# RWKV key norms summed token-major and turned back, in the input projection of a hybrid encoder layer

## The reference

```python
prev = jnp.pad(ub, ((0, 0), (1, 0), (0, 0)))[:, :-1]
ub = ub + (prev - ub) * mu                       # token shift
r, k, v, w_low, a_low, g_low = _split(ub, B_COLS)
...
a = jax.nn.sigmoid(a0 + a_low @ a_up)
...
kk = _l2norm(_heads(k * k_k, RWKV_HEADS))        # u * rsqrt(sum(u * u) + 1e-6) over the 64 columns of a head
k = k * (1.0 + (a - 1.0) * k_a)
...
bonus = jnp.sum(r_h * k_h * r_k, -1, keepdims=True) * v_h
```

## Time and profile before

| | |
|---|---|
| median of 3 runs | 2105.22 us (2103.75 to 2105.71) |
| time of the profiled execution | 2102.6 us |
| its span, first to last instruction | 2100.8 us |
| mean granted TensorE clock | 0.974 |
| TensorE busy | 1967.7 us, 94% |
| VectorE busy | 1078.3 us, 51% |
| ScalarE, GpSimd busy | 567.8 us, 558.6 us |

### The profile page before, as it was taken

How to read it: one execution, slowest core, us unless ns; L and a number is a source line. 1 busy time by engine, 2 the same in 40 slices (tenths; PEclk the granted TensorE clock), 3 DMA queues, 4 the chain that set the end, 5 groups by cost and what they waited for, 6 DMA issues and landing times. The chain is left out here.

```text
span 2100.8 us, 29168 instructions
## 1 busy us (share of the span) xinstructions
PE 1967.7 (94%) x11664; PEld 1575.3 (75%) x11664; DVE 1078.3 (51%) x1354; ACT 567.8 (27%) x884; POOL 558.6 (27%) x353
## 2 busy tenths in 40 slices
PE   5998979999999999899888999999999999999994
PEld 4876758767788887777767777888888888888883
DVE  3665764468429900566657644724334243443437
ACT  2443332334421121333331121321121211212112
POOL 3111112121122322433314473422121221212113
PEclk9999989999999999899999999999999999999997
DMA  5243566135563393566464461211121211211002
GB/s 144 53 70 89 130 151 164 51 76 140 148 173 100 97 218 107 147 189 197 119 215 131 134 207 51 61 61 50 41 60 30 60 32 58 60 30 60 30 20 80
DMA packets 328054, 211.84 MB, mean 101 GB/s; under 512 B 154349, under 2 KB 298349, under 8 KB 325905
## 3 DMA queue, kind: packets, MB, share of 16 engines
q1 hardware_dynamic: 251760, 156.33, 27.3%
q10 hardware_dynamic: 75568, 54.04, 9.0%
q0 software_dynamic: 624, 0.05, 0.2%
HBM read 151.27 MB, written 59.06 MB: 100 GB/s over the span
## 5 line engine op out<-in xcount | busy, mean ns | idle before, releaser
L154 PE MATMUL bank<-xhi,w_hi 128*128 128x512 f32 x976 | 396.3, 406 | 2.9 <-DVE xlo L920 2.9
L155 PE MATMUL bank<-xlo,w_hi 128*128 128x512 f32 x976 | 387.6, 397 | 0.0
L156 PE MATMUL bank<-xhi,w_lo 128*128 128x512 f32 x976 | 387.0, 397 | 0.0
L432 POOL TENSOR_TENSOR w_lo<-w_raw,w_hi 128x1024 fp32r<-128x1024 f32 x61 | 163.3, 2678 | 640.5 <-ACT w_hi L783 640.5
L2212 DVE TENSOR_TENSOR bw_raw<-bw_raw,b_ps 128x512 f32<-128x512 f32 x42 | 28.9, 688 | 388.3 <-PE b_ps L156 380.0
L154 PEld LDWEIGHTS bank<-xhi,w_hi 128*128 128x128 f32 x976 | 184.9, 189 | 49.0 <-issue 3.5
L155 PEld LDWEIGHTS bank<-xlo,w_hi 128*128 128x128 f32 x976 | 185.0, 190 | 44.7 <-issue 2.4
L156 PEld LDWEIGHTS bank<-xhi,w_lo 128*128 128x128 f32 x976 | 184.6, 189 | 45.0
L2220 DVE TENSOR_TENSOR y<-y,f_ps 128x512 f32<-128x512 f32 x320 | 201.0, 681 | 0.7
L1755 POOL TENSOR_TENSOR bw_split<-ff_raw_down,ff_hi_down 128x1024 fp32r<-128x1024 f32 x22 | 53.4, 2426 | 527.3 <-ACT ff_hi_down L2013 527.3
L154 PE MATMUL f_ps<-ff_hi_down,ff_hhi 128*128 128x512 f32 x352 | 142.7, 405 | 3.6 <-DVE ff_hlo L2231 3.6
(11 more groups left out here) (324 smaller groups left out, 3462.6 us busy)
## 6 DMA issues: line engine op xcount, KB each, us to landing
w_raw<-in_w_in ACTq DMA_DIRECT2D x61, 512.0 KB, 4.2
op<-opnd SPq DMA_DIRECT2D x16, 1152.0 KB, 5.5
u<-work ACTq DMA_DIRECT2D x68, 256.0 KB, 4.1
b_gate<-u SPq DMA_DIRECT2D x24, 512.0 KB, 3.6
ff_raw_gate<-in_ffn_gate SPq DMA_DIRECT2D x22, 512.0 KB, 4.0
ff_raw_up<-in_ffn_up SPq DMA_DIRECT2D x22, 512.0 KB, 5.3
ff_raw_down<-in_ffn_down SPq DMA_DIRECT2D x22, 512.0 KB, 5.9
opnd<-work SPq DMA_DIRECT2D x20, 512.0 KB, 6.2
```

What stands on the lines that cost most here:

```text
L154: pe.matmul(out, w_hi, x_hi, start=first, stop=False)
L155: pe.matmul(out, w_hi, x_lo, start=False, stop=False)
L156: return pe.matmul(out, w_lo, x_hi, start=False, stop=last)
L432: pool.tensor_tensor(w_lo[b][:, :, :], w_raw[b][:, :, :], as_f32(w_hi[b][:, :, :]), ALU.subtract).then_inc(w_lo_done, 1)
```

## The change

In the RWKV groups the squared keys are summed with the tokens on the output's partitions: for each block of 128 tokens a product with the block as the stationary side and two columns of `head_ones` as the moving one, so 16 columns hold all norms. ScalarE takes their square root, VectorE inverts 128x16 values, ScalarE widens them to 128x1024 with a copy, and TensorE turns them back with eight transposes into `z_ps`, from which VectorE multiplies `kk`. The product stands at `base[j] + 5` instead of `+ 6`. The token shift is computed as `raw * (1 - mu)` and then `prev * mu +` that. TensorE's low-rank product of the next group waits for `bonus_done` instead of `norm_done` and `outs`. The first diagonal product goes from `base[j] + 3` to `+ 4`; the second stays at `+ 5`, now behind the norm product. SyncE issues `store_blocks(j)` for j < 3 before the first turned `k` of the same group, where it stood behind all of them.

```diff
--- before.py
+++ after.py
@@ -167,7 +167,7 @@
     at = 0
     for name, n in (("mu", 14), ("w0", 4), ("a0", 4), ("k_k", 4), ("k_a", 4), ("r_k", 4), ("lnx_w", 4),
                     ("lnx_b", 4), ("conv", 48), ("norm_w", 1), ("a_log", 1), ("dt_bias", 1), ("sinks", 4),
-                    ("one_minus_k_a", 4), ("minus_a", 1), ("eps_q", 1), ("eps_k", 1), ("eps_gdn", 1), ("eps_lnx", 1), ("eps_ln", 1)):
+                    ("one_minus_k_a", 4), ("minus_a", 1), ("eps_q", 1), ("eps_k", 1), ("eps_gdn", 1), ("eps_lnx", 1), ("eps_ln", 1), ("one_minus_mu", 14)):
         PARAMS[name] = (at, n)
         at += n
     return at
@@ -348,6 +348,7 @@
         w_lo = [sb(f"w_lo{b}", [P, KT, P], F32R) for b in range(2)]
         low_up = [sb(f"low_up{b}", [P, P]) for b in range(4)]
         turned_tile = [sb(f"turned{b}", [P, 4, P]) for b in range(2)]
+        norm = sb("rw_norm", [P, 16])
         el, gc_col = sb("row_el", [GH, NCH]), sb("gc_col", [P, NCH, 2])
         bank = [local.enter_context(nc.psum_tensor(f"bank{b}", [P, HALF], F32)) for b in range(4)]
         z_ps, a_ps = (local.enter_context(nc.psum_tensor(n, [P, 2, HALF], F32)) for n in ("z_ps", "a_ps"))
@@ -377,6 +378,7 @@
         diag_mm, masked, nt_stored = sem("diag_mm"), sem("masked"), sem("nt_stored")
         along_landed, along_ready, along_exp = [sem(f"along_landed{n}") for n in range(4)], sem("along_ready"), sem("along_exp")
 
+        norm_inverse, norm_wide, norm_turned, bonus_done = (sem("rw_norm_" + n) for n in ("inverse", "wide", "turned", "bonus"))
         eg_landed = sem("eg_landed")
         taps_done, conv_done, silu_done, g_sq_done, g_norm_mm, g_norm_done, g_outs = (
             sem("g_" + n) for n in ("taps_done", "conv_done", "silu_done", "sq_done", "norm_mm", "norm_done", "outs"))
@@ -497,6 +499,9 @@
                             sp.wait_ge(mm_done, turned_by("rwkv", 2, "v"))
                             load_along(beta_along, R_BETA, 0)
                         n, g, slot = item[2], item[3], turn_slot[item]
+                        if kind == "rwkv" and j < 3 and (n, g) == ("k", 0):
+                            sp.wait_ge(masked, 2 * j + 2)
+                            store_blocks(j, rw(j)["n"])
                         sp.wait_ge(evac, done_at[item])
                         for half in range(2):
                             src = turned_tile[slot][rwkv_rows(half), :, :]
@@ -522,9 +527,6 @@
                         sp.dma_start(xinv[:, 32 * k:32 * k + 32, 2, u_, :].rearrange("c p t -> p c t"),
                                      chunks(n)[32 * k:32 * k + 32, :, NB:2 * NB]).then_inc(nt_stored, 16)
                 for j in range(4):
-                    if j:
-                        sp.wait_ge(masked, 2 * j)
-                        store_blocks(j - 1, rw(j - 1)["n"])
                     store_rwkv(j)
                     if j == 2:
                         sp.wait_ge(rw_stored[0], 224)
@@ -646,25 +648,30 @@
                     if j == 0:
                         pe.wait_ge(wa_done, 1)
                     else:
-                        pe.wait_ge(norm_done, j)
-                        pe.wait_ge(outs, j)
+                        pe.wait_ge(bonus_done, j)
                     for h in range(2):
                         cols_ = slice(h * HALF, (h + 1) * HALF)
                         pe.matmul(z_ps[:, h, :], low_up[j][0:64, :], wa[0:64, cols_], start=True, stop=True)
                         last = pe.matmul(a_ps[:, h, :], low_up[j][64:128, :], wa[64:128, cols_], start=True, stop=True)
                     last.then_inc(low_done, 1)
                     if j:
-                        yield from until(base[j] + 3)
+                        yield from until(base[j] + 4)
                         diag_rwkv(j - 1, 0)
-                        yield from until(base[j] + 5)
-                        diag_rwkv(j - 1, 1)
-                    yield from until(base[j] + 6)
+                    yield from until(base[j] + 5)
                     pe.wait_ge(sq_done, j + 1)
                     pe.wait_ge(sig_done, 2 * j + 2)
-                    whole(z_ps, tab("head_ones"), t["sq"], norm_mm)
+                    for n in range(8):
+                        last = pe.matmul(z_ps[:, 0, 2 * n:2 * n + 2], t["sq"][:, n * P:(n + 1) * P], tab("head_ones")[:, 0:P:RD], start=True, stop=True)
+                    last.then_inc(norm_mm, 1)
+                    if j:
+                        diag_rwkv(j - 1, 1)
                     yield from until(base[j] + 7)
                     pe.wait_ge(rk_done, j + 1)
                     whole(a_ps, tab("head_ones"), t["rk"], rk_mm)
+                    pe.wait_ge(norm_wide, j + 1)
+                    for n in range(8):
+                        last = pe.transpose(z_ps[:, n // 4, n % 4 * P:(n % 4 + 1) * P], t["nrm"][:, n * P:(n + 1) * P], tab("ident"))
+                    last.then_inc(norm_turned, 1)
                 for j in range(4):
                     yield from rwkv(j)
                 for half in range(2):
@@ -822,10 +829,13 @@
                     act.activation(t["a"], flat(a_ps), ACT.Sigmoid, bias=par("a0", j)).then_inc(sig_done, 1)
                     act.wait_ge(kk0_done, j + 1)
                     act.activation(t["sq"], t["kk"], ACT.Square).then_inc(sq_done, 1)
+                    yield from until(base[j] + 6)
+                    act.wait_ge(norm_mm, j + 1)
+                    act.activation(norm[:, :], z_ps[:, 0, 0:16], ACT.Sqrt, bias=par("eps_k")).then_inc(norm_done, 1)
                     yield from until(base[j] + 7)
-                    act.wait_ge(norm_mm, j + 1)
                     act.wait_ge(lc_done, j + 1)
-                    act.activation(t["nrm"], flat(z_ps), ACT.Sqrt, bias=par("eps_k")).then_inc(norm_done, 1)
+                    act.wait_ge(norm_inverse, j + 1)
+                    act.activation(t["nrm"].rearrange("p (n d) -> p n d", d=RD), norm[:, :].unsqueeze(2).to_broadcast([P, 16, RD]), ACT.Copy).then_inc(norm_wide, 1)
                     act.activation(t["ep"], t["lp"], ACT.Exp).then_inc(exp_done, 1)
                     act.activation(t["en"], t["lc"], ACT.Exp, scale=-1.0).then_inc(exp_done, 1)
                     act.activation(t["ec"], t["lc"], ACT.Exp).then_inc(exp_done, 1)
@@ -909,8 +919,8 @@
             def shift(n, tile, out, mu, scratch):
 
                 arrived(tile)
-                step(dve.tensor_tensor(scratch, raw(n, 1), raw(n), ALU.subtract))
-                step(dve.scalar_tensor_tensor(out, scratch, par("mu", mu), raw(n), ALU.mult, ALU.add))
+                step(dve.tensor_scalar(scratch, raw(n), par("one_minus_mu", mu), None, ALU.mult))
+                step(dve.scalar_tensor_tensor(out, raw(n, 1), par("mu", mu), scratch, ALU.mult, ALU.add))
                 dve.sem_inc(raw_read[n], 1)
 
             for n in range(16):
@@ -922,6 +932,7 @@
             for n in range(3):
                 dve.sem_inc(raw_read[n], 1)
             dve.wait_ge(par_landed, par_loads)
+            step(dve.tensor_scalar(par("one_minus_mu", 0, 14), par("mu", 0, 14), -1.0, 1.0, ALU.mult, ALU.add))
             step(dve.tensor_scalar(par("one_minus_k_a", 0, 4), par("k_a", 0, 4), -1.0, 1.0, ALU.mult, ALU.add))
             for name, value in (("eps_q", GD * L2_EPS), ("eps_k", L2_EPS), ("eps_gdn", GDN_EPS), ("eps_lnx", LNX_EPS), ("eps_ln", LN_EPS)):
                 step(dve.memset(par(name), value))
@@ -988,13 +999,15 @@
                 step(dve.tensor_scalar(t["d"], t["r"], par("r_k", j), None, ALU.mult))
                 dve.tensor_tensor(t["rk"], t["d"], t["k"], ALU.mult).then_inc(rk_done, 1)
                 dve.wait_ge(rk_done, j + 1)
+                dve.wait_ge(norm_done, j + 1)
+                dve.reciprocal(norm[:, :], norm[:, :]).then_inc(norm_inverse, 1)
                 shift(2, U_RV + j, t["v"], j + 8, t["d"])
-                dve.wait_ge(norm_done, j + 1)
-                step(dve.reciprocal(t["nrm"], t["nrm"]))
-                dve.tensor_tensor(t["kk"], t["kk"], t["nrm"], ALU.mult).then_inc(kk_done, 1)
+                dve.wait_ge(norm_turned, j + 1)
+                dve.tensor_tensor(t["kk"], t["kk"], flat(z_ps), ALU.mult).then_inc(kk_done, 1)
                 dve.wait_ge(kk_done, j + 1)
                 dve.wait_ge(rk_mm, j + 1)
-                step(dve.tensor_tensor(t["bonus"], flat(a_ps), t["v"], ALU.mult))
+                dve.tensor_tensor(t["bonus"], flat(a_ps), t["v"], ALU.mult).then_inc(bonus_done, 1)
+                dve.wait_ge(bonus_done, j + 1)
                 dve.wait_ge(exp_done, 3 * j + 3)
                 step(dve.scalar_tensor_tensor(t["ep"], t["kk"], -1.0, t["ep"], ALU.mult, ALU.mult))
                 step(dve.tensor_tensor(t["a"], t["kk"], t["a"], ALU.mult))
```

## The result

| | before | changed |
|---|---|---|
| median | 2104.49 us (4 runs) | 2071.64 us (2069.75 to 2073.28, 4 runs) |
| ratio, 95% interval | | 0.985 [0.9838, 0.9862] |
| span of the profiled execution | 2100.8 us | 2071.1 us |
| mean granted clock | 0.974 | 0.982 |

The forecast was 2069 us.

What follows compares the result with a forecast made beforehand. TensorE's instruction row in the input projection was taken as the bound: -38.6 + 0.7 + 2.0 = -35.9, so 2102.6 becomes 2066.7, and the median, 2.6 above, 2069 us. Own range 2062 to 2076; high end 2088 with (a) and (b).

Steps and rivals of the forecast that it cites:

- The loss of 38.6 us: TensorE in the input projection's RWKV groups: all time lost to stops and low clock, 38.6 us, taken as removable.
- seven stops: TensorE standing still in seven places of the RWKV groups, waiting for `outs` or on SyncE's store queue: 26.7 us.
- the 9.8 us: TensorE's loss at the lower clock between half-tile 13 and the last diagonal product, beside the stops: 9.8 us.
- the eight products with two moving columns: Norm products on TensorE per group: taken as 1.0 us, bounds 0.27 and 1.87; net norm term +0.7 in all.
- The new stop: TensorE at the third turn of group 3, waiting behind a late turned store: 2.0 us (0 to 4.5).
- 36.5 less 0.7: Between half-tile 13 and the last diagonal product: 36.5 us lost before, less 0.7 of added norm work.
- a gain of 2.1: Behind the last diagonal product: product, turn and half-tile take 9.2 us before, instead of 7.1.
- The covers: Slack before TensorE waits: 1.5 us for `sq`, 3.6 at the transposes; each GpSimd meeting costs up to 2.0.
- (a): Rival: a new stop at the wide copy or the square keeps part, +7 to +16, about 2080 us; chance 0.20.
- (b): Rival: clock falls without a TensorE stop in the cluster of product, transposes and turn, 2081 us; chance 0.07.
- (c): Rival: gain lost behind the projection, or stops only move from `outs` to `norm_wide`, 2100 to 2106 us; chance 0.03.
- (d): Rival: slower, TensorE waits in each group for a round trip through ScalarE and VectorE, 2108 us; chance 0.04.

Runs made afterwards that it cites:

- diagonal products back: Changed kernel with the diagonal products at their old places, first half at base + 3, second ahead of the norm product: 2070.77 us, ratio 0.9853.
- store back: Changed kernel with the masked blocks stored again behind all turned stores of a group: 2080.18 us, ratio 0.9891.
- norms as before: Changed kernel with the old norms (one head_ones product, wide square root, wide reciprocal), product behind half-tile base + 6: 2071.89 us, ratio 0.9862.
- low-rank waits for `outs`: Changed kernel, but TensorE's low-rank product waits for `outs` of the group before instead of `bonus_done`: 2076.76 us, ratio 0.987.
- waits and places only: Kernel before, with only the low-rank product waiting for `bonus_done` and the first diagonal product at base + 4: 2089.06 us, ratio 0.9934.

## Why the prediction was right

- **The loss of 38.6 us.** All seven stops went, and the low clock with them: 1.00 through the four groups, as the forecast asked for. But some 1.4 of the 9.8 us that the forecast put down to the clock were a remainder of its sum and not clock. With the norm parts as measured the same sum gives 173.0 us between the marks (169.3 - 4 x 1.71 + 4 x 2.64), and the changed kernel, without a stop there and at full clock, takes 174.4.
- **What was mis-sized: the eight products with two moving columns.** I took 1.0 us "slightly over the transposes' 0.88". They take 1.77, near the bound from above, 1.87. The term is +3.7, not +0.7. The ground was wrong, not only the number: the transposes carry the same weights in one record each, these products in two, and each record costs 0.11 us.
- **The new stop** was forecast at 2.0 behind the third turn of group 3. It is there with 0.7. First ScalarE's evacuation of that turn, then the half-tile that waits for it:

```profile
305.89 0.60 ACT L783 ACTIVATE turned<-bank 128x512 f32<-128x512 f32 x1 [5.84 <-PE bank L620]
```

```profile
306.63 0.47 PE L154 MATMUL bank<-xhi,w_hi 128*128 128x512 f32 x1 [0.74 <-ACT turned L783]
```

The turn named as the releaser had ended at 300; what came last was the store of the tile's earlier contents. SyncE's turned stores of the group began at 301.69, and 305.89 is 4.2 us behind, as the forecast had it from the earlier trace rows. What was shorter than forecast is the way to it: from the group's first store at 285.67 it is 16.0 us, where 17.7 had been counted.
- **The balance.** Between the marks 35.8 us were forecast (36.5 less 0.7) and 31.3 came. Of the missing 4.5, 3.1 are the norm products. The other 1.4 are the remainder named above. They lie in joints between parts that I counted as free: a half-tile with its turn, for one, takes 6.10 behind a diagonal product (158.94 to 165.04) and 6.04 between two turns. In the medians the forecast was -35.9 and the result -32.9. That the miss is no larger owes something to luck: behind the second mark the forecast had a gain of 2.1 and a stop of 2.0; measured were 1.0 gained with the stop in it, and 1.3 lost again in later parts, where the cause stays open (+0.3 in all).

- **The covers held.** The worst meeting with GpSimd, at 210.65, stretched a pass of 1.22 to 3.24 and the path to the transposes had room for it:

```profile
210.65 3.24 DVE L996 TENSOR_TENSOR decays<-decays 128x1024 f32<-128x1024 f32 x1
```

- **What the forecast left open.** It credited the shorter norm and the earlier wait together, without asking what each is worth when the other is there. The total came out right all the same, since it was counted from the stops and not from the parts.
- **Rivals.** (a), a wait at the wide copy or the square, did not come: between the norm product and the transposes TensorE never waits. (b), a clock that falls in the cluster of small products, did not come in the changed kernel: product, transposes and turn stand back to back at 180 to 183 us and the clock is 1.00. It is no idle rival, though: with the diagonal products back at their old places the clock fell once behind such a cluster, without a stop, and cost 1.5 us. The Trainium skill's page "TensorE: Matmul & The Clock Gate", section "Part 4: PE-mode transpose", has it that transposes do not count as busy in the same way. No trace here can tell: eight transposes in group 0 and twelve in each other group, 1.3 us, stand between dense matmuls and take nothing from the clock, but in the kernel before real stops of 1.45 and 1.68 us took nothing from it either. (c) and (d) did not come; behind the last mark both kernels take the same time.

## What to carry to other kernels

When several edits attack one stop, price each with the others in place: a wait that names an earlier link of a chain and a chain that is shorter pay for much of it only once. Then ask what the dearer one still adds (here 3.4 us between the marks, 3.7 of work already taken off). Before a wide vector operation is shrunk by a detour over TensorE, count the loads of the stationary side, not the columns that move. And look where stores stand in a DMA queue relative to the buffer that waits for them: moving six issues forward was worth 9 to 12 us here between the marks, and cost at most the new stop of 0.7.

## What the runs showed of the hardware

A float32 matmul with 2 moving columns and a new stationary block of 128 columns took 0.22 us and left two records; with 64 moving columns it took 0.23 (1.82/8). A transpose of a 128x128 block took 0.11 and left one.

What a stop costs in clock did not go by its length. Of lost clock, its share in the stop itself included, a stop of 0.6 us had 1.7 us (0.83 over 10 us, store back), one of 2.7 also 1.7 (0.89 over 15 us, norms as before), one of 3.2 as much (0.83 over 10 us, low-rank waits for `outs`), one of 5.6 had 3.5 (0.86 over 25 us), and one of 5.0 had 3.6 (0.91 over 40 us). Stops of 0.7 (changed), 0.9 (store back), 1.2 (diagonal products back), 1.45 and 1.68 (before) and 2.8 us (waits and places only) had none (1.00). And once the clock fell without a stop (0.84 over 10 us, diagonal products back). So a removed stop's share of clock can't be priced ahead from its length alone.
